# VectorE's order at two places of a two-block kernel: the first scan's products ahead of the first unit's rest, and the second mixer's softplus between a block's taps

## The reference

```python
# first block
proj = x @ w_in                       # q, k, v, z_att, z_ssm, xbc, dt_raw
xbc = silu(causal_depthwise_conv(xbc, conv_w, conv_b))
dt = softplus(dt_raw + dt_bias);  a = -exp(a_log)
# chunks of 128 tokens, two groups of 8 heads
y_diag = einsum(cb * decay, x * dt)
states = einsum(b, (x * dt) * decay_to_end)
y = y_diag + y_off + d_skip * x
out = concat(y_att, rms_norm(y * silu(z_ssm))) @ w_out
x = layer_norm(alpha * x + out)
# second block (gated delta rule)
qkv, z, b_lin, a_lin = split(h @ w_in_2)
qkv = silu(causal_depthwise_conv_2(qkv, conv_w_2))     # 4096 channels, 4 taps
beta = sigmoid(b_lin)
g = -exp(a_log) * softplus(a_lin + dt_bias)
```

## Time and profile before

| | before |
|---|---|
| median of 3 runs | 1103.57 us (1103.26 to 1104.26) |
| the profiled execution | 1103.89 us |
| its span (first to last instruction) | 1102.1 us |
| TensorE busy | 1059.9 us, 96% |
| VectorE busy | 661.8 us, 60% |
| ScalarE busy | 442.9 us, 40% |
| GpSimd busy | 210.4 us, 19% |
| start of the output stage | about 384 us |
| block `b == 1` of the second mixer on VectorE | 591.9 to 616.7 us |

### The profile page before, as it was taken

One profiled execution on the slowest core, in us unless ns is written; L12 is line 12 of the kernel. 1 busy time (PEld: TensorE's weight loads), 2 busy tenths in 40 slices (PEclk: granted clock), 3 DMA queues, 4 the chain that ended last, 5 costly groups with the idle time before them and its releaser, 6 DMA issues. The chain is left out here.

```text
span 1102.1 us, 14438 instructions
## 1 busy us (share of the span) xinstructions
PE 1059.9 (96%) x5558; PEld 872.8 (79%) x5558; DVE 661.8 (60%) x1137; ACT 442.9 (40%) x824; POOL 210.4 (19%) x159
## 2 busy tenths in 40 slices
PE   7999999999999999999899999999999998999997
PEld 4888888888779877788778788887878876888885
DVE  4245435742156597765736865666595667976635
ACT  4223224342266562231623334348623447325432
POOL 0010000000000052201300100002104754045792
PEclk9999999999989999999899999999999999999999
DMA  8276634322041050232324345435221222203401
GB/s 301 78 274 210 220 95 147 114 84 95 8 146 59 3 195 3 74 134 77 125 77 153 115 152 192 153 115 172 78 76 33 103 96 78 77 20 105 183 1 77
DMA packets 58306, 123.89 MB, mean 112 GB/s; under 512 B 5760, under 2 KB 6016, under 8 KB 58112
## 3 DMA queue, kind: packets, MB, share of 16 engines
q1 hardware_dynamic: 55792, 110.22, 29.5%
q0 software_dynamic: 2304, 12.58, 3.2%
q10 hardware_dynamic: 144, 0.20, 0.1%
HBM read 108.83 MB, written 14.16 MB: 112 GB/s over the span
## 5 line engine op out<-in xcount | busy, mean ns | idle before, releaser
L287 DVE TENSOR_TENSOR w_lo<-raw,w_hi 128x2048 fp32r<-128x2048 f32 x58 | 135.6, 2337 | 211.1 <-ACT w_hi L283 200.1
L283 ACT ACTIVATE w_hi<-raw 128x2048 fp32r<-128x2048 f32 x51 | 97.6, 1914 | 211.7 <-PE projections_ps L131 138.3
L129 PE MATMUL projections_ps<-projections_x_hi,w_hi 128*128 128x512 f32 x208 | 81.1, 390 | 0.4 <-ACTq L503 0.4
L131 PE MATMUL projections_ps<-projections_x_hi,w_lo 128*128 128x512 f32 x208 | 81.0, 389 | 0.0
L130 PE MATMUL projections_ps<-projections_x_lo,w_hi 128*128 128x512 f32 x208 | 80.9, 389 | 0.0
L131 PE MATMUL projections_ps<-w_hi,projections_x_lo 128*128 128x512 f32 x192 | 74.7, 389 | 0.0
L130 PE MATMUL projections_ps<-w_lo,projections_x_hi 128*128 128x512 f32 x192 | 74.7, 389 | 0.0
L129 PE MATMUL projections_ps<-w_hi,projections_x_hi 128*128 128x512 f32 x192 | 74.7, 389 | 0.0
L244 DVE SCALAR_TENSOR_TENSOR resid<-resid,mixer_cw 128x512 f32<-128x512 f32 x96 | 64.9, 745 | 0.0
L2428 POOL TENSOR_TENSOR mixer_es<-masks,mixer_gsel 128x1024 f32<-128x1024 f32 x8 | 17.3, 2165 | 230.0 <-PE mixer_ps L1890 152.1
L129 PE MATMUL output_ps<-w_hi,output_m_hi 128*128 128x512 f32 x128 | 53.2, 416 | 0.8 <-DVE output_m_lo L1257 0.7
(11 more groups left out here) (324 smaller groups left out, 2560.5 us busy)
## 6 DMA issues: line engine op xcount, KB each, us to landing
raw<-in_w_in SPq DMA_DIRECT2D x26, 1024.0 KB, 5.0
raw<-in_gdn_w_in SPq DMA_DIRECT2D x24, 1024.0 KB, 5.0
tok<-in_ada_w POOLq DMA_DIRECT2D x16, 768.0 KB, 6.3
raw<-in_w_out SPq DMA_DIRECT2D x8, 1024.0 KB, 5.0
qkv_kept<-mixer_ring SPq DMA_DIRECT2D x8, 1024.0 KB, 4.2
mixer_st<-qkv_kept SPq DMA_DIRECT2D x32, 256.0 KB, 2.9
raw<-in_gdn_w_out SPq DMA_DIRECT2D x8, 1024.0 KB, 5.1
resid<-in_att_bias SPq DMA_DIRECT2D x16, 256.0 KB, 2.6
```

Of the source, the lines that this page charges most:

```text
L129: nc.tensor.matmul(out, w_hi, x_hi, start=first, stop=False, skip_group_check=True)
L131: return nc.tensor.matmul(out, w_lo, x_hi, start=False, stop=last, skip_group_check=True)
L283: self.nc.scalar.activation(self.hi[s][:], self.raw[s][:], ACT.Copy).then_inc(self.hi_ready, 1)
L287: engine.tensor_tensor(self.lo[s][:], self.raw[s][:], self.hi[s][:], ALU.subtract)\
```

## The change

Two pieces of VectorE's program are written at another place; the instructions, their operands and their sizes are the same, and no other engine's program changes.

```diff
-            rest(0)
+            dve.wait_ge(decays_ok, 1)
+            own.did(nc.vector.tensor_tensor(dte[:], dt[:], decays[:, 1], ALU.mult))
             for e in range(4):
                 low(e)
-            dve.wait_ge(decays_ok, 1)
-            own.did(nc.vector.tensor_tensor(dte[:], dt[:], decays[:, 1], ALU.mult))
             own.wait()
+
             steps_of(0)
+            rest(0)
             for e in range(4, KT):
                 low(e)
             rest(1)
...
                 for pair in range(2):
                     conv.sum_taps(dve, b, pair)
-                if b == 1:
-                    soft_steps.finish(dve).then_inc(g_ok, 1)
-                    dve.wait_ge(beta_step, 1)
-                    nc.vector.tensor_scalar(beta[:], beta[:], 1.0, None, ALU.add).then_inc(beta_step, 1)
-                    dve.wait_ge(beta_step, 2)
-                    nc.vector.reciprocal(beta[:], beta[:]).then_inc(beta_step, 1)
-                    select(0)
+                    if b == 1 and pair == 0:
+
+                        soft_steps.finish(dve).then_inc(g_ok, 1)
+                        dve.wait_ge(beta_step, 1)
+                        nc.vector.tensor_scalar(beta[:], beta[:], 1.0, None, ALU.add).then_inc(beta_step, 1)
+                        dve.wait_ge(beta_step, 2)
+                        nc.vector.reciprocal(beta[:], beta[:]).then_inc(beta_step, 1)
+                        select(0)
```

## The result

The changed kernel takes 1110.64 us (median of 6 runs, 1108.87 to 1113.52), the kernel before 1103.84 us in the runs beside it; the ratio is 1.0065, with a 95% interval from 1.0053 to 1.0077. So it is 7 us slower. The forecast was 1105.3 us, its range ended at 1108.7, and "slower by over 0.2%", which is what came, had been given a chance of 0.27.

A forecast was written before the change was run, and what follows sets the result against it. The prediction took TensorE, busy for nearly the whole span, to bound the kernel. Its terms, -1.45 + 3.14 = +1.69 us, put on 1103.57 us, gave 1105.3 us, with a range of 1103.2 to 1108.7 us.

The forecast's parts named there:

- the clock behind the longer wait: Second mixer, rival: TensorE's 4.3 us wait makes its clock fall, costing 2.3 us, total 1107.6 us; chance 0.15.
- place one: Output stage, VectorE reordered: TensorE starts the second unit of group(0) at 400.27 instead of 401.72, -1.45 us.
- the held taps: Second mixer: GpSimd's product holds the second pair's taps on VectorE, +1.83 us, bounds 0 and 1.9 us.
- place two: Second mixer, softplus chain moved between the two pairs' taps: +3.14 us, from +1.3 to +3.2 us.
- the race with GpSimd: Output stage, rival: GpSimd's product goes ahead of unit 0's w_lo; total 1106.7 us or 1108.6 us; chance 0.07.
- The series at place two: Second mixer: chain, taps, silus, rounding and w_lo run in series, so TensorE starts at 620.43 against 619.12, +1.31 us.
- the one that already waits is served: VectorE and GpSimd excluding each other: when both ask again, the engine already waiting goes first; no size of its own.
- dense products ahead: Second mixer: argument against a clock fall, the products ahead of the wait being dense ones of 512 columns, not small.
- Carried to the end: After the output stage: TensorE has work without a gap there and everything follows it, so the 1.45 us gain lasts.
- scatter of half a us: Whole kernel: scatter allowed in the forecast case's own range, 1104.2 to 1105.8 us.

The follow-up runs named there:

- place one alone: Kernel before with only the output stage's new VectorE order, the second mixer as before: 1104.05 us, ratio 1.0001.
- split chain: Changed kernel with the second mixer's softplus chain cut into three parts, placed where VectorE was idle: 1102.95 us, ratio 0.9988; timed again 1102.88 us, 0.9993.
- GpSimd held: Changed kernel with GpSimd's first log decay product and memsets waiting for all taps of block 1: 1108.31 us, ratio 1.0040.
- chain between the units: Changed kernel with the softplus chain moved between the w_lo of block 2's two units: 1105.59 us, ratio 1.0014.
- rounding first: Changed kernel with ScalarE rounding block 2's first unit ahead of the silus of block 1's second pair: 1108.16 us, ratio 1.0039.
- split chain alone: Kernel with the softplus chain in three parts but the output stage as in the kernel before: 1105.70 us, ratio 1.0010.

## Why the prediction was wrong, step by step

The steps that failed are two that the sum had at nothing: the clock behind the longer wait, left to a rival with a chance of 0.15, and the work behind 838 us, which was taken to be as long as before. Together they are some 4 us of the 6.0 us (7.7 - 1.7) by which the mean span grew more than forecast. The term of place one makes another 1.45 us of it in that mean, and the held taps 0.3 to 0.6.

- **Place one, -1.45 us: right at one course of the clock only.** It was worked out from one profile, which shows one of two cases. The same stretch in the second profile of before, VectorE and TensorE, and the clock share of the first and of the second profile over 384 to 392 us:

```profile
392.89 0.39 DVE L1341 TENSOR_TENSOR output_dte<-dt,output_decays 128x64 f32<-128x64 f32 x1
...
394.66 0.66 PE L991 MATMUL output_ps<-masks,xbc 128*128 128x128 f32 x4 [0.98 <-DVE output_xdte L1270]
```

```profile
384.00:392.00 8.00, 7.55 (x32) 6.96 (x33) 5.56 (x4) 5.75 (x8) 4.89 (x4) 0.57 0.81 303
```

```profile
384.00:392.00 8.00, 7.53 (x40) 6.18 (x41) 5.55 (x5) 6.13 (x9) 5.76 (x5) 0.79 0.80 308
```

  In the first profile TensorE ran at half clock for nearly the whole stretch (0.57), line 1005 came late, GpSimd's product started only at 392.82 and held `dte` for 1.93 us. With 0.79 the product starts at 391.30 and `dte` takes 0.39 us. The kernel before then reaches its second unit 400.21 - 384.44 = 15.77 us behind GpSimd's first product, the changed one 15.81 us: VectorE does the same work in either order, and in the new one TensorE waits 0.70 and 1.11 us for `low` and `w_lo` in place of 0.98 us ahead of line 991. The gain of 1.5 us exists only in the first case. All eighteen profiles bear this out, whatever stands in the second mixer:

| output stage | share, 384 to 392 us | profiles | second unit behind GpSimd's first product | start to line 1775 |
|---|---|---|---|---|
| old order | 0.57 to 0.58 | 3 | 17.1 to 17.3 | 539.8 to 540.0 |
| new order | 0.57 to 0.58 | 5 | 15.7 to 15.9 | 538.4 to 538.8 |
| old order | 0.67 to 0.70 | 2 | 17.1 to 17.2 | 538.0 and 538.4 |
| new order | 0.70 | 1 | 15.7 | 536.6 |
| old order | 0.79 | 2 | 15.8 | 538.5 and 539.8 |
| new order | 0.79 | 5 | 15.8 | 538.6 to 539.9 |

  Locally, then, the forecast -1.45 us was about right where the old order meets a share of 0.57 to 0.70, as in five of its seven profiles: the new one comes to line 1775 some 1.3 to 1.6 us earlier there. Where the share is 0.79, there is nothing to gain. In the totals it does not show as such: place one alone is 0.3 us above before in the mean, and beside place two and beside the split chain the kernels with place one are 1.1 us and 1.9 us below those without (1110.86 against 1111.96, 1102.89 against 1104.77). What the clock does elsewhere moves the totals by more than this term. Of the details, the race with GpSimd was lost in the changed kernel's first profile (`w_lo` 3.13 us, the product first at 392.30), which the prediction had given 0.07 and priced at 1.4 us or more. In the new order it is lost in the five profiles with 0.79 and won in the other six, where `w_lo` takes 2.28 us. The price was wrong: won or lost, the second unit starts 15.7 to 15.9 us behind GpSimd's first product.
- **The series at place two, +1.31 us: right.** 1.23 us with GpSimd out of the way.
- **The taps held, +1.83 us: right in kind, the size off by a race.** 2.47 us in two of three profiles (3.44 - 0.97) and 1.55 in the third (2.52). The upper bound of 1.9 us was too low, because the memset behind the product can hold a tap as well. The prediction also said that of two waiting engines the one that already waits is served; a tap has waited since before the product ended, and still the memset goes first in four of the six profiles with this order (3.43 or 3.44 us). The prediction counted nothing for the memsets, and for the tap that was wrong: where the memset goes first the two taps take 3.44 us, and where it comes behind them 2.52 us. For `w_lo` it would have been right: the memset runs beside the first of two with GpSimd held, and they take 4.49 us as with nothing beside them.
- **The clock behind the wait: a rival with 0.15 that came in every profile.** Its condition, a wait near 4.4 us, was met in two of three profiles, and the third had 4.01 us. The price named was 2.3 us. Measured: 5.3 us between the rows (302.6 of the first profile against 297.3 of the second and third of before, which have the same half clock behind line 1775), less 3.78 us of longer wait, is 1.5 us. In the third profile, with the shorter wait, the share of the clock over 620 to 628 us was 0.58 and the fall cost some 2.5 us; an estimate, from the same 5.3 us less 2.86 (4.01 - 1.15). The argument against it, dense products ahead, had no row behind it, and the clock fell behind 2.38 us too (0.85 over 612 to 620 us).
- **Carried to the end: the step that failed unnamed.** The sum took for granted that 1 us at 620 us is 1 us at the end. Behind 838 us stand places where TensorE is busy with small products and short waits, and whether its clock falls there differs from run to run and from kernel to kernel: its share over 836 to 860 us is 1.00, 0.93 and 1.00 in the three profiles of before, and 1.00, 0.86 and 0.93 in those of the changed kernel. That cost another 2.1 us in the profiles of the changed kernel, and 2.7 us in the kernel of before that was only made 5.46 us later. No term or bound of the prediction held it.

In sum: forecast -1.45 + 3.14 = +1.7 us. In the means of three profiles each came 0 up to line 1775, 3.5 for the longer wait, some 2 for the clock beside it, and 2.1 for later falls; 7.7 together. That the clock's part is only partly the change's doing, since the kernel before has such falls in one of three profiles, was not in the forecast's scatter of half a us either.

## What to carry to other kernels

One profile shows one course of the clock: before a wait of a us or two is sold as a gain, profile the kernel again and see whether the wait, and the contention that makes it, are there at both courses (here shares of 0.57 and of 0.79 over 384 to 392 us). Work taken from a place where it lay beside another engine's work is not moved for free: look for what will stand in series with it (here silus, rounding, `w_lo`), and for which of its last instructions releases an engine that holds the next ones (here GpSimd, beside whose product and memset two taps took 3.44 us in place of 0.97). A chain of short instructions is best cut to the length of the idle gaps that it goes into; here the 7 us of loss went, and the kernel came out some 0.8 to 1.3 us below before (ratios of 0.9993 and 0.9988). It is the fastest of these kernels, but 1 lies inside both intervals, so a gain over the kernel before is not shown.

## What the runs showed of the hardware

- `dte`, of 64 elements in SBUF, ends 0.08 us behind the end of GpSimd's product in all seven profiles with the old output stage, and takes from 0.39 us (second profile of before, from 392.89, the product ending at 391.30 + 1.90 = 393.20) to 1.93 us (the first). In the same seven the first `w_lo` takes 3.88 us, with GpSimd's two products beside its start, against 2.28 us undisturbed. `E` takes 2.92 us behind GpSimd's product and 1.23 us with nothing of GpSimd beside it (before, 401.59 and 405.94), and the copy of 32 elements near 900 us takes 0.68 us where it takes 0.20 us at 616.52. GpSimd's product takes 1.90 us, and is listed with 3.88 us where it is issued during a `w_lo` (chain between the units: 620.57, the `w_lo` ending at 622.69).
- The four `low`, which read PSUM, take 2.71 us with GpSimd's product beside them for 1.67 us (second profile of before, 390.26 to 392.97), and 2.72 us with no instruction of GpSimd beside them (GpSimd held, 386.46 to 389.18).
- A `tensor_scalar` of 128x512 in SBUF is held by GpSimd's product (two take 2.52 us in place of 0.97) and by a GpSimd memset, which reads nothing (3.44 us); a `tensor_tensor` with two SBUF inputs is held by the first (3.13 us in place of 2.28) and not by the second (4.49 us for two).
- Which of two waiting engines comes next differs between runs of the same kernel: 2.52 or 3.44 us for the same two taps. In four of six profiles the memset went ahead of a tap that already waited.
- TensorE's clock fell from a share of 1.00 to one half in or right behind waits of 4.9, 4.0 and 2.38 us (0.79 and 0.58 over 620 to 628 us, 0.85 over 612 to 620 us), and stayed at 1.00 at waits of 1.43, 2.34 (twice) and 1.15 us (over 612 to 620 us for the first two, 636 to 648 us for the chain between the units, 616 to 620 us for the first profile of before). It also fell near 846 us with no wait above 0.6 us around it (0.86 over 841.3 to 865.3 us).
- With nothing changed but 5.46 us of further products 150 us earlier, the time grew by 8.15 us; with 2.73 us, by 2.4 us. Single runs of one kernel spread over up to 7 us (rounding first, 1103.50 to 1110.54), and their mean clocks with them (split chain: 1100.6 to 1101.4 us at 0.987 to 0.992, 1102.8 to 1104.7 at 0.986, 1106.2 at 0.984).

What stays open is what decides, at the places near 842, 935 and 990 us, whether the clock falls, and so why the split chain alone is slower than the split chain with place one by more than place one can save.
